# Two weight units split by one instruction, decay steps spread over more blocks, attention logits and their maximum in one pass

## The reference, cut to what matters

```python
# GLA, per chunk of 64 tokens: decays within the chunk and over it
log_a = log_sigmoid(g_low @ w_gate_up + b_gate) / 16
cum = cumsum(log_a within a chunk); total = cum at the chunk's end
k_dec = k * exp(total - cum); chunk_decay = exp(total)
...
# second block, attention: 256 tokens are one block, so each query sees the keys up to its own position
s = (q * d_head ** -0.5) @ k.T + rel_table[bucket(distance)];  s = -inf above the diagonal
p = softmax(s);  o = p @ v
...
x = x + square(relu(norm(x) @ w_mlp_up)) @ w_mlp_down
```

## Time and profile before

| | |
|---|---|
| time, median of 3 runs | 2568.01 us (2566.7 to 2569.77) |
| the profiled execution's own time | 2568.39 us |
| its span | 2566.6 us |
| TensorE busy (matmuls) | 2546.3 us, 99% |
| VectorE busy | 1815.6 us, 71% |
| ScalarE busy | 1348.3 us, 53% |
| DMA engines busy with the weight queue | 62.6% |
| HBM read | 499.69 MB, 196 GB/s over the span |
| granted TensorE clock, mean | 0.997 |

### The profile page before, as it was taken

One profiled execution on the slowest core, in us unless ns is written; L12 is line 12 of the kernel. 1 busy time (PEld: TensorE's weight loads), 2 busy tenths in 40 slices (PEclk: granted clock), 3 DMA queues, 4 the chain that ended last, 5 costly groups with the idle time before them and its releaser, 6 DMA issues.

```text
span 2566.6 us, 43594 instructions
## 1 busy us (share of the span) xinstructions
PE 2546.3 (99%) x15628; PEld 2336.8 (91%) x15628; DVE 1815.6 (71%) x2067; ACT 1348.3 (53%) x1635; POOL 95.8 (4%) x96
## 2 busy tenths in 40 slices
PE   9999999999999999999999999999999999999998
PEld 8889999999999999999899999999999999999997
DVE  6767877667666677866897666766777676676675
ACT  6546555444444455544675555555554444454454
POOL 1000020000000002200000000000110000000001
PEclk9999999999999999999999999999999999999999
DMA  7794666666666666775556666666666666666664
GB/s 231 169 207 147 201 202 200 204 199 202 198 197 204 202 198 197 220 216 179 165 173 210 198 202 201 196 196 206 203 198 202 198 196 204 196 202 204 199 200 144
DMA packets 507427, 504.65 MB, mean 197 GB/s; under 512 B 17907, under 2 KB 505608, under 8 KB 507336
## 3 DMA queue, kind: packets, MB, share of 16 engines
q1 hardware_dynamic: 506060, 501.79, 62.6%
q10 hardware_dynamic: 1276, 1.63, 1.5%
HBM read 499.69 MB, written 3.67 MB: 196 GB/s over the span
## 4 chain that ended last, share of the span: by engine, by line
PE 94%; DMA 3%; DVE 2%; ACT 1%; issue 0%; SPq 0%; DVEq 0%; ACTq 0%
PE acc L545 60%; PE acc L547 30%; DMA raw<-in_gla_w_in 3%; PE acc L540 2%; DVE wsp L1157 1%; PE acc L542 1%; DVE lat L1490 0%; ACT wsp L835 0%; DMA xtok<-in_x 0%; PE misc L658 0%; PE misc L673 0%; PE misc L776 0%; PE misc L627 0%; PE misc L675 0%; DVE lat L1486 0%
## 5 line engine op out<-in xcount | busy, mean ns | idle before, releaser
L1157 DVE TENSOR_TENSOR wsp<-raw,wsp 128x1024 fp32r<-128x1024 f32 x944 | 1164.7, 1245 | 491.1 <-ACT wsp L835 456.9
L545 PE MATMUL acc<-xs,wsp 128*128 128x512 f32 x4224 | 1394.0, 383 | 3.5 <-DVE wsp L1157 3.0
L835 ACT ACTIVATE wsp<-raw 128x1024 fp32r<-128x1024 f32 x944 | 991.9, 1058 | 610.2 <-PE acc L547 506.2
L547 PE MATMUL acc<-xs,wsp 128*128 128x256 f32 x4224 | 1151.5, 273 | 0.0
L545 PEld LDWEIGHTS acc<-xs,wsp 128*128 128x128 f32 x4224 | 798.7, 189 | 116.7 <-DVE wsp L1157 5.0
L545 PE MATMUL acc<-hs,wsp 128*128 128x512 f32 x2560 | 841.0, 382 | 0.0
L547 PEld LDWEIGHTS acc<-xs,wsp 128*128 128x128 f32 x4224 | 811.2, 192 | 0.4
L547 PE MATMUL acc<-hs,wsp 128*128 128x256 f32 x2560 | 697.8, 273 | 0.0
L545 PEld LDWEIGHTS acc<-hs,wsp 128*128 128x128 f32 x2560 | 483.9, 189 | 67.2
L547 PEld LDWEIGHTS acc<-hs,wsp 128*128 128x128 f32 x2560 | 491.5, 192 | 0.0
L1167 DVE TENSOR_TENSOR z<-acc,corr 128x512 f32<-128x512 f32 x246 | 200.2, 814 | 184.6 <-ACT corr L846 184.5
(11 more groups left out here) (243 smaller groups left out, 1051.6 us busy)
## 6 DMA issues: line engine op xcount, KB each, us to landing
raw<-in_w_in SPq DMA_DIRECT2D x224, 512.0 KB, 4.4
raw<-in_mlp_w_up SPq DMA_DIRECT2D x128, 512.0 KB, 4.0
raw<-in_mlp_w_down SPq DMA_DIRECT2D x128, 512.0 KB, 4.3
raw<-in_w_mlp_up SPq DMA_DIRECT2D x128, 512.0 KB, 4.0
raw<-in_w_mlp_down SPq DMA_DIRECT2D x128, 512.0 KB, 4.3
raw<-in_gla_w_in SPq DMA_DIRECT2D x96, 512.0 KB, 4.8
raw<-in_gla_w_out SPq DMA_DIRECT2D x32, 512.0 KB, 4.5
raw<-in_w_out SPq DMA_DIRECT2D x32, 512.0 KB, 3.8
```

The source lines that it names most:

```text
L545: pe.matmul(both, w_part(0, slot)[:, t, cols], taking_turns(x[:, k0 + k]), start=start, stop=False, skip_group_check=True)
L547: ins = pe.matmul(acc[:, g, j, 1], w_part(1, slot)[:, t, cols], taking_turns(x[:, k0 + k, 0]), start=False, stop=stop, skip_group_check=True)
L835: act.activation(w_part(0, slot), raw[:, slot], ACT.Copy).then_inc(hi_done, 1)
L1157: dve.tensor_tensor(w_part(1, slot), raw[:, slot], w_part(0, slot).bitcast(F32), ALU.subtract).then_inc(lo_done, 1)
```

## The change

1. **Pairs.** `in_twos` looks at the units of the next round that are split ahead of a block's end. If the first two are in neighbouring slots, ScalarE makes both high parts in one instruction, and VectorE both low parts in one; counters go up by 2. That pair waits for both loads, and for TensorE to be done with both slots. The first rounds (before block gk1) and the last unit of a block stay single.
2. **Decay steps.** The scan is done in two halves, in gv2 and gv3; the step of gv3 moves to gv4, the multiplication of the keys from gv4 to gv6, the last small steps from gv6 to gv7; ScalarE's Exp of both moves from gv3 to gv5.
3. **Logits.** The scale AD ** -0.5 is applied to q when it is stored. The bias is added and the row maximum taken by one `tensor_tensor_reduce` per piece, in place of an add pass and a maximum pass each.

The change's short description also says "no throwaway passes". The diff takes out no other instruction; the spare matmuls are as before.

```diff
-    def w_part(k, slot):
+    def w_part(k, slot, units=1):
         n = UK * NB
         start = HIGHS + k * LOWS + slot * n
-        return wsp[:, start:start + n].rearrange("p (t n) -> p t n", t=UK)
+        return wsp[:, start:start + units * n].rearrange("p (t n) -> p t n", t=units * UK)
+
+    def raw_part(slot, units):
+        return raw[:, slot:slot + units].rearrange("p s t n -> p (s t) n")
+
+    def in_twos(ahead):
+        (r, s), (r1, s1) = ahead[0], ahead[1] if len(ahead) > 1 else (None, None)
+        if s1 == s + 1:
+            return [(r, s, 2)] + [(r2, s2, 1) for r2, s2 in ahead[2:]]
+        return [(r2, s2, 1) for r2, s2 in ahead]
...
-        def split_hi(rnd, slot):
+        def split_hi(rnd, slot, units=1):
             if is_past_end(rnd):
                 return
-            act.wait_ge(raw_landed[slot], 16 * (rnd + 1))
+            for k in range(units):
+                act.wait_ge(raw_landed[slot + k], 16 * (rnd + 1))
             if not (isinstance(rnd, int) and rnd == 0):
-                act.wait_ge(unit_used, SLOTS * (rnd - 1) + slot + 1)
-            act.activation(w_part(0, slot), raw[:, slot], ACT.Copy).then_inc(hi_done, 1)
+                act.wait_ge(unit_used, SLOTS * (rnd - 1) + slot + units)
+            act.activation(w_part(0, slot, units), raw_part(slot, units), ACT.Copy).then_inc(hi_done, units)
...
             ahead = look_ahead(rnd, first, n)
-            for r, s in ahead[:-1]:
-                split_hi(r, s)
+            for r, s, units in in_twos(ahead[:-1]):
+                split_hi(r, s, units)
...
-            if (name, i) == ("gv", 3):
+            if (name, i) == ("gv", 5):
                 act.wait_ge(suffix_done, 1)
                 act.activation(lat[:], lat[:], ACT.Exp, scale=1.0 / TEMP).then_inc(suffix_exp, 1)
...
-        def split_lo(rnd, slot):
+        def split_lo(rnd, slot, units=1):
             if is_past_end(rnd):
                 return
-            dve.wait_ge(hi_done, SLOTS * rnd + slot + 1)
-            dve.tensor_tensor(w_part(1, slot), raw[:, slot], w_part(0, slot).bitcast(F32),
-                              ALU.subtract).then_inc(lo_done, 1)
+            dve.wait_ge(hi_done, SLOTS * rnd + slot + units)
+            dve.tensor_tensor(w_part(1, slot, units), raw_part(slot, units), w_part(0, slot, units).bitcast(F32),
+                              ALU.subtract).then_inc(lo_done, units)
...
-            for r, s in look_ahead(rnd, first, n)[:-1]:
-                split_lo(r, s)
+            for r, s, units in in_twos(look_ahead(rnd, first, n)[:-1]):
+                split_lo(r, s, units)
...
-            if (name, i) == ("gv", 6):
+            if (name, i) == ("gv", 7):
                 softplus_rest()
...
-            if (name, i) == ("gv", 2):
+            if name == "gv" and i in (2, 3):
                 dve.wait_ge(zero_done, 3)
-                fl = [t[:].rearrange("p k t -> p (k t)") for t in (mn, segm, lat)]
+                part = slice((i - 2) * LKT // 2, (i - 1) * LKT // 2)
+                fl = [t[:, part].rearrange("p k t -> p (k t)") for t in (mn, segm, lat)]
                 own.done(dve.tensor_tensor_scan(fl[0], fl[1], fl[2], 0.0, ALU.mult, ALU.add))
-            if (name, i) == ("gv", 3):
+            if (name, i) == ("gv", 4):
...
-            if (name, i) == ("gv", 4):
+            if (name, i) == ("gv", 6):
                 dve.wait_ge(suffix_exp, 1)
...
-                dve.scalar_tensor_tensor(out=attn[:, 0:P], in0=flat[1][:, 0:P], scalar=AD ** -0.5, in1=skew[:, s, P:T],
-                                         op0=ALU.mult, op1=ALU.add)
-                own.done(dve.scalar_tensor_tensor(out=attn[:, P:BW], in0=flat[1][:, P:BW], scalar=AD ** -0.5,
-                                                  in1=skew[:, s], op0=ALU.mult, op1=ALU.add))
-                dve.tensor_reduce(amax[:, 0:1], attn[:, 0:P], AX_X, ALU.max)
-                own.done(dve.tensor_reduce(amax[:, 1:2], attn[:, P:BW], AX_X, ALU.max))
+                dve.tensor_tensor_reduce(attn[:, 0:P], flat[1][:, 0:P], skew[:, s, P:T], 1.0, NEG, ALU.add, ALU.max, amax[:, 0:1])
+                own.done(dve.tensor_tensor_reduce(attn[:, P:BW], flat[1][:, P:BW], skew[:, s], 1.0, NEG, ALU.add, ALU.max,
+                                                  amax[:, 1:2]))
...
-                scaled(pair(q2 if name == "q" else k2, i)).then_inc(qkv_ready, 1)
+                scaled(pair(q2 if name == "q" else k2, i), AD ** -0.5 if name == "q" else 1.0).then_inc(qkv_ready, 1)
```

## The result

The changed kernel takes 2614.05 us (median of 4, 2613.1 to 2615.8) against 2568.69 (4 runs): ratio 1.018, 95% interval 1.0168 to 1.0193. Slower, as forecast, but by 45.4 us and not by 22.5, and beyond the range of 2564 to 2606. The profiled execution spans 2611.4 us against 2566.6.

The account below looks back on a forecast made before the run. TensorE makes nine tenths of the chain; slot 2's load rounds from 85.32 to 170.07 us are the main movable share. Terms 20 + 1 + 1.5 = 22.5 us on 2568.4 us, 0.4 over the median, gave 2591 us, range 2564 to 2606.

Parts of the forecast that it names:

- Prices of a pair: High pair 1916 ns, low pair 2285 ns, 4.2 us in all; 0.2 us saved per engine in some 220 blocks, worth 0.
- Bias-write stretch, +20: In gv to gq both loads of each pair fall behind a bias write every round, costing 20 us.
- 10.9 + 1.9 + 1.3 = 14.1 us: Time between bias writes: load landing after the write, high pair, then slot 2's high part start to next write; before, 12.1.
- Some 0.7 us remain ... 0: First MLP block: pair done at 511.8, TensorE starts its next block at 512.62, so no cost.
- 1 us to spare: Steady blocks: the pair's two loads land at 517.1, needed at 518.06, so no cost.
- Rival 4: Steady slack absent: each 0.1 us missed costs 20 us over some 200 blocks; 2600 to 2640 us, chance 0.07.
- gr4 +1.0: At block gr4 TensorE starts at 260.10 after one low part; a pair is done at 261.07, costing 1.0 us.
- the convolution +1.5: Convolution blocks: pairs and fused logits give +0.2 for each of three rounds and +1.05 once; bounds -1 and +4.
- the lower of the two bounds: Fused logits pass costs what the add pass cost, saving 0.65 us per head; the other bound saves nothing.
- Decays 0: Spread decay steps remove stalls of 0.73 and 3.07 us and 1.7 us of clock, but gain 0 beside the load chain.
- the chain's cover: Slot 2's load chain, 85.32 to 170.07 us, contains neither decay stall; without that cover the gain would be 5.5 us.
- Rival 1: Pair loads get past the bias write and land within 6 us in gv2; 2559 to 2563 us, faster, chance 0.14.

Follow-up runs that it names:

- spaced: Changed kernel with 14 matmuls of 512 columns (3.1 us) added on TensorE after each of the blocks gv1 to gq0: 2620.17 us.
- looped: Changed kernel with TensorE's six blocks gv2 to gv7 written as a loop of three passes of two blocks, instructions fetched once: 2612.31 us.
- late_hi_only: Changed kernel with single units in gk to gr; from go to the end ScalarE keeps pairs, VectorE takes units singly: 2570.19 us.
- logits_rows128: Kernel before plus fused logits only, bias rows written once to DRAM and copied there, 128 rows a copy: 2559.09 us.
- logits_one_write: Kernel before plus fused logits only, with all eight bias rows issued as one write from eight partitions: 2580.10 us.
- singles_one_write: Changed kernel without pairs, with all eight bias rows issued as one write from eight partitions: 2577.54 us.
- singles_rows128: Changed kernel without pairs, bias rows written once to DRAM and copied there, 128 rows a copy: 2559.62 us.

## Why the prediction was right or wrong

- **Prices of a pair**: right, 1914 and 2297 ns against 1916 and 2285 forecast, 222 of each.
- **Bias-write stretch, +20**: that the pair's loads fall behind the write, round after round, was right; the size was off. Forecast was a round of 10.9 + 1.9 + 1.3 = 14.1 us. A short round is 14.2 to 14.3, but that is luck: the pair starts 11.7 us after the write, and the next write goes out only 2.6 us later (84.22, 95.96, 98.55), two errors that cancel. The 1.3 us from the start of a high part to the next write is no wait of its own; the write leaves when slot 3's load has landed. Missing was the instruction packet in three of seven rounds, 1.2 us each, and behind the last write, where the pair starts after 13.0 us. 7 x (14.74 - 14.1) + 2.1 is 6.6 of the 7.2 us that were missed. That packets do it rests on the landings in the rounds with and without one, here and in `spaced`; that the clock isn't needed for it, on `spaced`. `looped` shows long rounds by the clock alone (0.66 in the block of 156.94), so without the packets not all of the 1.2 us would have come back.
- **"Some 0.7 us remain ... 0" and "1 us to spare" in the steady blocks**: this step failed. It was put at 0 and measured 14.8 us (m1 5.5, m2 4.3, mix 3.1, br 1.1, q 0.8), two thirds of the 22.6 us by which the sum was short. The block that was costed does hold; the error was to let one undisturbed block stand for 200. Wherever something comes ahead of the pair that takes longer than the margin of 0.7 us, a table load (1.28 us), the norm's steps (ScalarE idle 3.34 us ahead of them), a late load (5.10 us of ScalarE's wait at 2434.45), TensorE waits for the low pair; with single low parts (`late_hi_only`) 0.6 us of this loss are left. Rival 4 named the lack of slack, but as a loss in every block.
- **gr4 +1.0 and the convolution +1.5**: right, 1.1 and 1.5; the parts too (logits -1.9 against 3 x -0.65, pairs +3.4 against 3 x 0.86 + 1.05 = +3.6; these terms add up to 1.7, not to the 1.5 that the prediction wrote down). The fused pass costs what the add pass cost (419 and 282 ns against 415 and 284), the lower of the two bounds; a short read of 0.08 us comes behind each and mostly overlaps, and from the first pass to the negation a head takes 0.67 us in place of 1.30.
- **Decays 0**: right value, wrong reason. The two stalls were put down to the long decay steps, with 5.5 us to be had if the chain's cover were gone (3.8 us, and 1.7 us of the block whose granted clock was 0.86). `logits_rows128` has those steps without the chain, and TensorE doesn't stand still. The stalls seem to need loads that are late already: with the one write, which makes them late, the long steps cost 2.4 us in gv3 and gv4 (`logits_one_write` against `singles_one_write`).
- **Rival 1**, by which the loads get past the write or run between its packets: here they did not. In every round they landed in the order of issue, all behind the write; after the write of 84.22 no packet of them starts before 91.81 us, 1.0 us before the write's last packet ends.

## What to carry to other kernels

One instruction for two units saved 0.2 us here on either engine (1.91 us against 2 x 1.06, 2.30 against 2 x 1.25), but delays the first unit, and all that its buffer sets free, by the length of the second: cost it in the worst block of a stage, not in a typical one, and let the engine that frees the buffer go on unit by unit. The broadcast write of 192 KB out of one partition took 8.8 us, and for 7.6 us after its issue (84.22 to 91.81) no packet of a load behind it started; of the four ways measured the copies from DRAM by 128 rows (sixteen landings, 4.5 us; TensorE without a gap in `singles_rows128`) were the cheapest, while with 127 rows (two landings, 13 to 19 us) gv7 and gq0 took 13.4 and 14.1 us. A stall beside a chain belongs to a step only if it stays when the chain is gone.

## What the runs showed of the hardware

- The same 192 KB took 8.8 us from one partition, 5.2 from 128, 4.5 from one row in DRAM by 128 rows (medians from issue to landing); 127 rows, with two landings in place of sixteen, took 13 to 19. One packet of 1.5 KB took 0.77 us from the one partition (median of 1024 in the changed kernel) and 0.07 us in the other three.
- The packet of 16 KB of instructions in each of the changed kernel's long rounds took 0.93 to 0.96 us; the 59 of its whole trace took 0.88 to 2.60 us. In those rounds the loads behind it landed 1.0 to 1.4 us later than in the short ones; one that came 1.1 us ahead of slot 3's landing, in `looped`, delayed nothing (slot 3 landed 1.36 us after slot 2). With pairs, edits in gv to gq alone (`spaced`, `looped`) added 4.7 us of stalls in m1 and q.
